# A hybrid retention/attention block on one Trainium2 core: a GpSimd adding transfer issued later, two slab loads swapped, and a VectorE norm put ahead of a slab sum

## The chip, the cores and the metric

One Trainium2 chip, one of its cores, one launch. The metric is the device time of the whole program in microseconds (us), lower is better. "Before" is the kernel as it stood, "after" the kernel with the diff below. All times are from the hardware profiler or from the device's own timing of a run.

## The reference, cut to what matters

```python
h    = rms_norm(x, norm1_g)                     # x: 256 x 2048, float32
proj = h @ w_in                                 # 2048 x 7168; columns: retention q,k,v,gate, attention q,k,v; 8 heads of 128 each
A = silu(gate) * head_group_norm(retention(rotary(q), rotary(k), v))
B = chunk_attention(rms_norm(aq), rms_norm(ak), av, rel_bias)     # chunks of 64 frames, softmax
x = x + concat(A, B) @ w_out                    # 2048 x 2048
x = x + square(relu(rms_norm(x, norm2_g) @ w_ff1)) @ w_ff2        # 2048 x 8192, 8192 x 2048
```

## The kernel before, in words

**Split products.** Every product is made in three: each float32 operand is split into a high part (fp32r) and a low part, and the matmuls high*high, low*high and high*low are added in PSUM. So every weight slab goes through four hands: SP (SyncE) issues its load into one of five raw buffers, ScalarE (ACT) writes the rounded copy `w_hi` (line 1095 in the first phase), VectorE (DVE) writes `w_lo = raw - w_hi` (line 1557), and TensorE (PE) does the matmuls of lines 840 and 847 (with `w_hi`) and of line 853 (with `w_lo`). A slab is four 128-row tiles, and is worked on in two halves called pieces, numbered q in the order of use.

**Phases.** The first phase, about 0 to 370 us, is the projection by `w_in`, head pair by head pair, with retention and attention of the finished heads between its pieces. Then come the product by `w_out` and the feed-forward. The change is in the first phase only.

**Blocks.** The first phase has four blocks of two heads, 0 to 3, and a remainder. `IN_STARTS` holds each block's first piece: 0, 26, 70, 114, 158. The function `at_piece(i, pos, f, ...)` puts a step f behind piece `IN_STARTS[i] + pos` in one engine's own order. ACT and DVE each run two pieces ahead (`AHEAD = 2`): at place q they first make the high or low half of piece q + 2 and then do the steps that are listed for q, in the order in which the lines list them. Each engine has such a list, and works it off strictly in order.

**Slab steps.** Within a block the slabs have names. I0 to I3 and J0 to J3 are the attention heads' slabs (384 columns), one set for each head. The retention pair's slabs are 512 columns wide and are multiplied in seven products instead of eight (Strassen's scheme): Q1 uses slab a, P5 uses a + b, P6 uses a + b + d, P7 uses b with a fourth slab added, P3 uses d, and so on. The same scheme in small letters (q1, p5, ...) serves a pair of attention heads. In blocks 1 to 3 the order of the last steps is I2 q2 Q1 I3 p4 P5 J2 P6 J3 P7 P3. These are at places 22 to 43 of the block, two places each, so J2 is at 34 and 35 and P6 at 36 and 37.

**Sums.** `in_sum(n, other, read)` on DVE adds a whole slab, 128x2048, to slab a (line 1566): first b, then d. The ACT copy of P6's first piece waits for the second of these sums (`in_summed >= 2 * pair + 2`). The fourth retention slab is added to b by a transfer that accumulates: `add_b` on GpSimd (POOL) waits for the first sum and then issues it (line 598); P7 waits for it to land. `add_e` does the same for slab a.

**Loads.** `IN_LOADS` is the order of SP's loads, and `in_plan` gives each the raw buffer that comes free first. Each load waits until DVE has made the low half of the last step that reads the buffer's earlier slab. In blocks 1 to 3 slab d waits for q2 and J2 waits for I3.

**Steps of the two heads.** Attention: ACT evacuates the projection with the scale 1/rms (`att_proj`, line 1115) and sums squares (`att_squares`, line 1131), DVE adds the epsilon (`att_mean_squares`, line 1645), POOL raises to the power -1/2 (`att_power`, line 588), DVE multiplies (`att_norm`, line 1650), PE transposes (`att_T`, line 701) behind place 35 of the block, directly ahead of P6. Retention of the second head of the pair before: `ret_power` on POOL (line 592) waits for statistics from DVE. The rotated q and k (`ret_rotated`, line 1696) are transposed by PE in `ret_T` (line 730).

**Block 0.** It has the same parts with fewer steps. The first norm's sums of squares of x are ACT's `x_squares` (line 1248); DVE's `x_mean_squares` and a POOL power make `rstd1`, which the first `att_proj` waits for. Product P5 is copied out of PSUM by `keep_in_p5` on ACT (line 1196).

Of the kernel before, what the change touches and what calls it, by code (L numbers as in the profile page):

```python
# [50 lines left out]
IN_STARTS = [0]  # L51
for _i in range(1, BLOCKS + 1):
    _r, _here = "Z1 Q2 Z2 P4 H1 H2", "Z1 Q2 q1 Z2 P4 p5 H1 p6 H2 p7 p3 I2 q2 Q1 I3 p4 P5 J2 P6 J3 P7 P3"
    _loads = "Z1 e A Z2 B D H1 H2 I2 E a I3 b d J2 J3" if _i < BLOCKS else "Z1 e Z2 H1 H2"
    IN_STARTS.append(2 * len(IN_ORDER))
    _before = ["Z1", "Q2", "Z2", "P4", "H1", "H2", "e"]
    IN_ORDER += [(_i - (step in _before), step) for step in (_here if _i < BLOCKS else _r).split()]
    IN_LOADS += [(_i - (name in _before), name) for name in _loads.split()]
# [28 lines left out]
def hybrid_block(nc, x, x_cols, w_att, w_ret, w_out, w_up, w_down, gains, rel_windows, rope_cos, rope_sin, decay, out):  # L87
# [3 lines left out]
    with ExitStack() as ctx:  # L91
# [486 lines left out]
        @block.gpsimd  # L578
        def _(pool):
            nc.gpsimd.memset(neg_half[:], -0.5).then_inc(half_ok, 1)  # L580
            nc.gpsimd.memset(ident[:], 0.0).then_inc(zeroed, 1)
            pool.wait_ge(zeroed, 1)
            nc.gpsimd.affine_select(out=ident[:], in_=ident[:], compare_op=ALU.not_equal, fill=1.0, base=0,
                                    pattern=[[-1, P]], channel_multiplier=1).then_inc(ident_ok, 1)

            def att_power(h):
                pool.wait_ge(a_ms_ok, h + 1)
                nc.gpsimd.tensor_tensor(a_rs[:], a_ms[:], neg_half[:], ALU.pow).then_inc(a_rs_ok, 1)

            def ret_power(u):  # L590
                pool.wait_ge(r_ve_ok, u + 1)
                nc.gpsimd.tensor_tensor(r_rs[:], r_ve[:], neg_half[:, 0:MT], ALU.pow).then_inc(r_rs_ok, 1)

            def add_second(n, into, c, done):

                table, cols = w_att if n % 2 else w_ret, SLAB_KT * pair_cols(n)
                row = pair_row(n, c, 1)
                nc.gpsimd.dma_start(raw[:, pair_raw(n, into)[0], 0:cols], table[row:row + P, :],
                                    accum_op=ALU.add).then_inc(done, 16)

            def add_b(n):
                pool.wait_ge(in_summed, 2 * n + 1)
                add_second(n, "b", 1, in_b)

            def add_e(n):
                pool.wait_ge(lo_done, pair_first(n, "P6") + 2)
                add_second(n, "a", 0, in_e)

            def mask_bias(i):
                pool.wait_ge(bias_in[i], 16)  # L610
                nc.gpsimd.memset(bias[0:CHUNK, 2 * i:2 * i + 2, P + CHUNK:2 * P], -1e30).then_inc(mask_ok, 1)

            add_b(0)
            pool.wait_ge(half_ok, 1)
            pool.wait_ge(me_ok, 1)
            nc.gpsimd.tensor_tensor(rstd1[:], me[:], neg_half[:, 0:MT], ALU.pow).then_inc(rstd1_ok, 1)
            att_power(0)
            mask_bias(0)
            add_e(0)
            att_power(1)  # L620
            for i in range(1, BLOCKS):
                add_b(2 * i - 1)
                add_e(2 * i - 1)
                ret_power(2 * i - 2)
                mask_bias(i)
                add_b(2 * i)
                ret_power(2 * i - 1)
                att_power(2 * i)
                add_e(2 * i)
                att_power(2 * i + 1)  # L630
            ret_power(HEADS - 2)
            ret_power(HEADS - 1)

            def add_slabs(p):

                table, first = weights(p)
                pool.wait_ge(summed, 2 * p + 1)
                row = ((first + 1) * SLABS + 1) * P
                nc.gpsimd.dma_start(raw[:, PLAN[p, "b"][0], :], table[row:row + P, :],
                                    accum_op=ALU.add).then_inc(b_summed, 16)  # L640
                pool.wait_ge(slab_lo, slab_no(p, "P6") + 1)
                row = (first * SLABS + 1) * P
                nc.gpsimd.dma_start(raw[:, PLAN[p, "a"][0], :], table[row:row + P, :],
                                    accum_op=ALU.add).then_inc(e_summed, 16)

            add_slabs(0)
            pool.wait_ge(me2_ok, 1)
            nc.gpsimd.tensor_tensor(rstd2[:], me2[:], neg_half[:, 0:MT], ALU.pow).then_inc(rstd2_ok, 1)
            for p in range(1, PAIRS):
                add_slabs(p)  # L650
# [6 lines left out]
        def _(pe):  # L657
# [213 lines left out]

            for h in range(HEADS):
                i, second = h // 2, h % 2
                places = ((23, 25, 27, 28), (29, 31, 34, 36))[second] if i == 0 else (
                    (35, 37, 41, 43), (46, 48, 51, 53))[second]
                for pos, f in zip(places, (att_T, att_scores, att_PT, att_pv)):
                    at_piece(i, pos, f, h)
# [188 lines left out]
        def _(act):  # L1066
# [191 lines left out]
            def at_piece(i, pos, f, *args):  # L1258
                work.setdefault(IN_STARTS[i] + pos, []).append(lambda: f(*args))

            for f, pos in enumerate((9, 11, 18, 20)):
                at_piece(0, pos, s_hi, f)
            for c, pos in enumerate((14, 15, 16, 17)):
                at_piece(0, pos, x_squares, c)
            at_piece(0, 12, keep_in_q1, 0)
            at_piece(0, 16, keep_in_p5, 0)
            at_piece(0, 18, att_proj, 0)
            at_piece(0, 20, att_squares, 0)
            at_piece(0, 22, att_proj, 1)
            at_piece(0, 23, att_qT, 0)  # L1270
# [5 lines left out]
            at_piece(0, 28, att_mix, 0)  # L1276
            at_piece(0, 30, att_qT, 1)
            at_piece(0, 32, att_exp, 1)
            at_piece(0, 35, att_pT, 1)
            at_piece(0, 37, att_mix, 1)  # L1280
            for i in range(1, BLOCKS):
                h, u, n = 2 * i, 2 * i - 2, 2 * i
                at_piece(i, 6, keep_in_q1, n - 1)
# [267 lines left out]
        def _(dve):  # L1551
# [17 lines left out]
            def in_sum_half(n, other, read, half):  # L1569
# [6 lines left out]
                if half:  # L1576
                    ins.then_inc(in_summed, 1)

            def set_z(n):

                dve.wait_ge(p5_kept, n + 1)
                dve.wait_ge(piece_used, pair_first(n, "P6") + 2)
                dve.wait_ge(acc_read_act, pair_reads(n) + 1)
                cols = slice(0, pair_cols(n))
                nc.vector.tensor_tensor(bZ[:, cols], in_p5[:, cols], bX[:, cols], ALU.subtract).then_inc(z_set, 1)
# [182 lines left out]
            def at_piece(i, pos, f, *args):  # L1768
                work.setdefault(IN_STARTS[i] + pos, []).append(lambda: f(*args))
# [6 lines left out]
                at_piece(0, pos, s_lo, f)  # L1776
            at_piece(0, 10, in_sum, 0, "b", "Q1")
            at_piece(0, 14, in_sum, 0, "d", "P5")
            at_piece(0, 17, x_mean_squares)
            at_piece(0, 19, set_z, 0)  # L1780
            at_piece(0, 19, s_lo, 2)
            at_piece(0, 20, att_mean_squares, 0)
# [6 lines left out]
            at_piece(0, 28, att_norm, 1)  # L1789
            at_piece(0, 32, att_bias_max, 1)  # L1790
            at_piece(0, 32, att_probs, 1)
            at_piece(0, 37, att_mix, 1)
            for i in range(1, BLOCKS):
                h, u, n = 2 * i, 2 * i - 2, 2 * i
                at_piece(i, 3, in_sum, n - 1, "b", "Q1")
                at_piece(i, 8, in_sum_half, n - 1, "d", "P5", 0)
                at_piece(i, 9, in_sum_half, n - 1, "d", "P5", 1)
                at_piece(i, 9, ret_rotate, u)
                at_piece(i, 11 if i == 1 else 10, ret_rotated, u)
                at_piece(i, 13, ret_kT, u)  # L1800
                at_piece(i, 14, ret_decay, u)
                at_piece(i, 16, set_z, n - 1)
                at_piece(i, 17, ret_norm, u)
                at_piece(i, 19, set_w, n - 1)
                at_piece(i, 20, ret_rotate, u + 1)
                at_piece(i, 21, ret_mix, u)
                at_piece(i, 21, ret_rotated, u + 1)
                at_piece(i, 24, ret_kT, u + 1)
                at_piece(i, 25, in_sum, n, "b", "Q1")
                at_piece(i, 26, ret_decay, u + 1)  # L1810
                at_piece(i, 29, ret_norm, u + 1)
                at_piece(i, 31, in_sum, n, "d", "P5")
                at_piece(i, 32, att_mean_squares, h)
                at_piece(i, 33, ret_mix, u + 1)
                at_piece(i, 34, att_norm, h)
                at_piece(i, 38, set_z, n)
                at_piece(i, 38, att_bias_max, h)
                at_piece(i, 40, att_probs, h)
                at_piece(i, 41, set_w, n)
                at_piece(i, 42, att_mean_squares, h + 1)  # L1820
                at_piece(i, 44, att_mix, h)
                at_piece(i, 44, att_norm, h + 1)
                at_piece(i, 49, att_bias_max, h + 1)
                at_piece(i, 50, att_probs, h + 1)
                at_piece(i, 54, att_mix, h + 1)
# [314 lines left out]
```

## Time and profile before

| | |
|---|---|
| median of 3 runs | 1103.39 us (1102.66 to 1103.53) |
| the profiled execution | 1103.28 us, span of the core 1101.1 us |
| PE busy | 1090.8 us (99%) |
| DVE busy | 885.7 us (80%) |
| ACT busy | 715.8 us (65%) |
| POOL busy | 59.2 us (5%) |
| granted TensorE clock | full in every slice |
| chain that ended last | PE 89%, DVE 3%, DMA 2%, ACT 1% |

The span is what the profile covers, from the first instruction to the last; the execution's time is 2.2 us more. Busy times of PE are of matmuls whose ends are modelled. An engine's idle time is put down to what ended it, and idle time of ACT, DVE or POOL costs nothing unless PE waits in its turn.

### The profile page before, as it was taken

The numbers are of one execution on the slowest core, as the hardware profiler recorded it, in microseconds if no ns is written. First come the engines' busy times: TensorE is split into PE (matmuls) and PEld (weight loads), VectorE is DVE, ScalarE is ACT, GpSimd is POOL, SyncE is SP. The second block draws the span as 40 slices with busy tenths as digits, with TensorE's granted clock in tenths as the row PEclk, the third lists the DMA queues.
The fourth block names the chain that finished last, engine by engine and source line by source line (L and its number), as shares of the span: only waits on it lengthen the run. The fifth ranks groups of instructions, "written<-read, shape, count | busy, mean of one in ns | idle before, by whom it ended". The sixth has DMA issues, their size and how long they took to land.

```text
span 1101.1 us, 13180 instructions
## 1 busy us (share of the span) xinstructions
PE 1090.8 (99%) x5154; PEld 925.1 (84%) x5154; DVE 885.7 (80%) x836; ACT 715.8 (65%) x857; POOL 59.2 (5%) x75
## 2 busy tenths in 40 slices
PE   9999999999999999999999999999999999999998
PEld 9788889889888888888888888888888888888887
DVE  7888878988976677969878779778869787869784
ACT  7876676776764456777755677655677655577662
POOL 0100100100100000000000000000000000000000
PEclk9999999999999999999999999999999999999999
DMA  9886776776756647778788788787787787787792
GB/s 362 298 262 218 214 261 218 227 249 229 226 211 252 256 159 219 257 249 251 230 282 244 253 267 231 229 302 223 249 285 217 238 290 223 258 278 220 246 279 91
DMA packets 44829, 268.53 MB, mean 244 GB/s; under 512 B 4960, under 2 KB 7776, under 8 KB 17120
## 3 DMA queue, kind: packets, MB, share of 16 engines
q1 hardware_dynamic: 37712, 220.61, 53.6%
q0 software_dynamic: 6624, 46.66, 22.4%
q8 instruction: 41, 0.67, 0.2%
q10 hardware_dynamic: 432, 0.41, 0.1%
q14 instruction: 20, 0.16, 0.0%
HBM read 265.57 MB, written 2.10 MB: 243 GB/s over the span
## 4 chain that ended last, share of the span: by engine, by line
PE 89%; DVE 3%; DMA 2%; ACT 1%; issue 1%; DVEq 0%; ACTq 0%
PE acc L972 10%; PE acc L968 10%; PE acc L970 10%; PE acc L840 5%; PE acc L847 5%; PE acc L853 5%; PE bankC L930 4%; PE bankC L923 4%; PE acc L930 4%; PE acc L923 4%; PE acc L925 4%; PE bankC L925 4%; DMA raw<-in_w_att 2%; PE acc L668 2%; PE acc L673 2%; PE acc L680 2%
## 5 line engine op out<-in xcount | busy, mean ns | idle before, releaser
L1867 DVE TENSOR_TENSOR w_lo<-raw,w_hi 128x2048 fp32r<-128x2048 f32 x180 | 410.9, 2288 | 127.2 <-ACT w_hi L1360 126.9
L1360 ACT ACTIVATE w_hi<-raw 128x2048 fp32r<-128x2048 f32 x180 | 344.7, 1916 | 219.8 <-PE acc L972 150.6
L1557 DVE TENSOR_TENSOR w_lo<-raw,w_hi 128x1024 fp32r<-128x1024 f32 (+1 forms) x168 | 180.8, 1093 | 36.9 <-ACT w_hi L1095 36.4
L1095 ACT ACTIVATE w_hi<-raw 128x1024 fp32r<-128x1024 f32 (+1 forms) x168 | 156.8, 954 | 39.6 <-PE acc L853 22.4
L968 PE MATMUL acc<-w_hi,hF_hi 128*128 128x512 f32 x256 | 100.8, 394 | 0.0
L972 PE MATMUL acc<-w_hi,hF_lo 128*128 128x512 f32 x256 | 99.8, 390 | 0.0
L970 PE MATMUL acc<-w_lo,hF_hi 128*128 128x512 f32 x256 | 99.7, 389 | 0.0
L968 PE MATMUL acc<-w_hi,dF_hi 128*128 128x512 f32 x248 | 96.8, 391 | 0.0
L972 PE MATMUL acc<-w_hi,dF_lo 128*128 128x512 f32 x248 | 96.5, 389 | 0.0
L970 PE MATMUL acc<-w_lo,dF_hi 128*128 128x512 f32 x248 | 96.5, 389 | 0.0
L840 PE MATMUL acc<-w_hi,hT_hi 128*128 128x384 f32 (+1 forms) x336 | 87.3, 374 | 3.0 <-ACT w_hi L1095 2.8
L847 PE MATMUL acc<-w_hi,hT_lo 128*128 128x384 f32 (+1 forms) x336 | 83.3, 362 | 0.0
L853 PE MATMUL acc<-w_lo,hT_hi 128*128 128x384 f32 (+1 forms) x336 | 83.0, 361 | 0.2 <-DVE w_lo L1557 0.2
L1875 DVE TENSOR_TENSOR raw<-raw 128x2048 f32<-128x2048 f32 x32 | 73.1, 2284 | 0.0
L840 PEld LDWEIGHTS acc<-w_hi,hT_hi 128*128 128x128 f32 x336 | 59.2, 188 | 9.8 <-ACT w_hi L1095 5.0
L853 PEld LDWEIGHTS acc<-w_lo,hT_hi 128*128 128x128 f32 x336 | 61.2, 188 | 7.1 <-DVE w_lo L1557 0.6
L847 PEld LDWEIGHTS acc<-w_hi,hT_lo 128*128 128x128 f32 x336 | 61.5, 188 | 6.8
L972 PEld LDWEIGHTS acc<-w_hi,hF_lo 128*128 128x128 f32 x256 | 48.1, 188 | 10.1
L968 PEld LDWEIGHTS acc<-w_hi,hF_hi 128*128 128x128 f32 x256 | 48.1, 188 | 9.8
L970 PEld LDWEIGHTS acc<-w_lo,hF_hi 128*128 128x128 f32 x256 | 48.1, 188 | 9.5
L972 PEld LDWEIGHTS acc<-w_hi,dF_lo 128*128 128x128 f32 x248 | 46.6, 188 | 9.7
L970 PEld LDWEIGHTS acc<-w_lo,dF_hi 128*128 128x128 f32 x248 | 46.6, 188 | 9.6
(278 smaller groups left out, 1903.1 us busy)
## 6 DMA issues: line engine op xcount, KB each, us to landing
raw<-in_w_up SPq DMA_DIRECT2D x64, 1024.0 KB, 6.2
raw<-in_w_down SPq DMA_DIRECT2D x64, 1024.0 KB, 6.5
raw<-in_w_ret SPq DMA_DIRECT2D x32, 1024.0 KB, 6.0
raw<-in_w_att SPq DMA_DIRECT2D x28, 768.0 KB, 5.8
raw<-in_w_out SPq DMA_DIRECT2D x16, 1024.0 KB, 4.8
raw<-in_w_up POOLq DMA_DIRECT2D x16, 1024.0 KB, 9.1
raw<-in_w_down POOLq DMA_DIRECT2D x16, 1024.0 KB, 8.7
raw<-in_w_ret POOLq DMA_DIRECT2D x8, 1024.0 KB, 9.2
```

Of the source, the lines that this page charges most:

```text
L840: nc.tensor.matmul(bank[:, 0:wide], stationary(step, m, t)[0], piece(w_hi, q, start, start + wide), start=fresh, stop=False, skip_group_ch ...
L847: nc.tensor.matmul(bank[:, 0:n], stationary(step, m, t)[1], piece(w_hi, q, start, start + n), start=False, stop=False, skip_group_check=True)
L853: mm = nc.tensor.matmul(bank[:, 0:n], stationary(step, m, t)[0], piece(w_lo, q, start, start + n), start=False, stop=t == SLAB_KT - 1, ski ...
L923: nc.tensor.matmul(bank[:], hi[:, form, tile_cols(t)], wh[:, cols], start=first and t == 0, stop=False, skip_group_check=True)
L925: nc.tensor.matmul(bank[:], lo[:, form, tile_cols(t)], wh[:, cols], start=False, stop=False, skip_group_check=True)
L968: nc.tensor.matmul(banks[m][:], hi[:, form + m, tile_cols(t)], wh[:, cols], start=False, stop=False, skip_group_check=True)
L970: nc.tensor.matmul(banks[m][:], hi[:, form + m, tile_cols(t)], wl[:, cols], start=False, stop=False, skip_group_check=True)
L972: mm = nc.tensor.matmul(banks[m][:], lo[:, form + m, tile_cols(t)], wh[:, cols], start=False, stop=t == SLAB_KT - 1, skip_group_check=True)
L1095: nc.scalar.activation(piece(w_hi, q, 0, n), raw[:, r, half * n:(half + 1) * n], ACT.Copy).then_inc(hi_done, 1)
L1360: nc.scalar.activation(w_hi[:, ring(s)], raw[:, r, :], ACT.Copy).then_inc(slab_hi, 1)
L1557: nc.vector.tensor_tensor(piece(w_lo, q, 0, n), raw[:, IN_PLAN[i, READ_AT.get(step, step)][0], half * n:(half + 1) * n], piece(w_hi, q, 0, ...
L1867: nc.vector.tensor_tensor(w_lo[:, ring(s)], raw[:, r, :], w_hi[:, ring(s)].bitcast(f32), ALU.subtract).then_inc(slab_lo, 1)
```

## The change

In block 0 it reorders ACT's steps between places 16 and 20, puts the copy of P5 on DVE (`keep_first_p5`), and moves the second head's `att_pT`, `att_pv` and `att_mix` one place forward. In blocks 1 to 3 it loads J2 ahead of d, issues `add_b` behind `ret_power` of the second head and behind the landing of J2, moves DVE's sum with d from place 31 to 33 and its `att_norm` from 34 to 33, ahead of that sum. In block 1 `ret_rotated` goes from place 11 to 10, as in the other blocks.

```diff
-    _loads = "Z1 e A Z2 B D H1 H2 I2 E a I3 b d J2 J3" if _i < BLOCKS else "Z1 e Z2 H1 H2"
+    _loads = "Z1 e A Z2 B D H1 H2 I2 E a I3 b J2 d J3" if _i < BLOCKS else "Z1 e Z2 H1 H2"
...
+            def slab_landed(i, name):
+                slot, loaded, _ = IN_PLAN[i, name]
+                pool.wait_ge(in_raw[slot], loaded)
...
                 mask_bias(i)
+                ret_power(2 * i - 1)
+                slab_landed(i, "J2")
                 add_b(2 * i)
-                ret_power(2 * i - 1)
                 att_power(2 * i)
...
-                places = ((23, 25, 27, 28), (29, 31, 34, 36))[second] if i == 0 else (
+                places = ((23, 25, 27, 28), (29, 31, 34, 35))[second] if i == 0 else (
...
-            for f, pos in enumerate((9, 11, 18, 20)):
+            for f, pos in enumerate((9, 11, 19, 20)):
                 at_piece(0, pos, s_hi, f)
-            for c, pos in enumerate((14, 15, 16, 17)):
+            for c, pos in enumerate((14, 15, 17, 18)):
                 at_piece(0, pos, x_squares, c)
             at_piece(0, 12, keep_in_q1, 0)
-            at_piece(0, 16, keep_in_p5, 0)
-            at_piece(0, 18, att_proj, 0)
+            at_piece(0, 19, att_proj, 0)
...
-            at_piece(0, 35, att_pT, 1)
-            at_piece(0, 37, att_mix, 1)
+            at_piece(0, 34, att_pT, 1)
+            at_piece(0, 36, att_mix, 1)
...
+            def keep_first_p5():
+                dve.wait_ge(piece_used, pair_first(0, "P5") + 2)
+                nc.vector.tensor_copy(in_p5[:], bF[:]).then_inc(p5_kept, 1)
...
-            at_piece(0, 17, x_mean_squares)
+            at_piece(0, 16, keep_first_p5)
+            at_piece(0, 18, x_mean_squares)
...
-            at_piece(0, 37, att_mix, 1)
+            at_piece(0, 36, att_mix, 1)
...
-                at_piece(i, 11 if i == 1 else 10, ret_rotated, u)
+                at_piece(i, 10, ret_rotated, u)
...
-                at_piece(i, 31, in_sum, n, "d", "P5")
                 at_piece(i, 32, att_mean_squares, h)
                 at_piece(i, 33, ret_mix, u + 1)
-                at_piece(i, 34, att_norm, h)
+                at_piece(i, 33, att_norm, h)
+                at_piece(i, 33, in_sum, n, "d", "P5")
```

## Rows read from the trace of the kernel before

**Rows 1.** Waits of PE, whole span: waiting line, releaser, total us, times, longest us.

```profile
PE acc L840 <- ACT w_hi L1095: 2.8, 3, 1.4
...
PE bankC L840 <- ACT w_hi L1095: 1.2, 1, 1.2
PE bankA L730 <- DVE r_qk L1696: 0.9, 1, 0.9
PE bankA L701 <- DVE a_qk L1650: 0.5, 1, 0.5
```

**Rows 2.** Timeline of PE, block 1, P5 to P6: start us, us, instructions, idle before.

```profile
121.88 0.63 PE L853 MATMUL bankD<-w_lo,sf_hi 128*128 128x512 f32 x2
123.94 0.97 PE L840 MATMUL acc<-w_hi,hT_hi 128*128 128x384 f32 x4 [1.43 <-ACT w_hi L1095]
...
128.59 0.71 PE L840 MATMUL bankC<-w_hi,sf_hi 128*128 128x512 f32 x2
```

**Rows 3.** Timeline of SP, block 1: issues of b and d, then of J2 and J3.

```profile
104.17 3.06 SPq L484 DMA_DIRECT2D raw<-in_w_ret  x2
114.31 2.06 SPq L484 DMA_DIRECT2D raw<-in_w_att  x2
```

**Rows 4.** Timeline of ACT, block 1, around the copy of J2.

```profile
120.76 0.19 ACT L1131 ACTIVATION_READ_ACCUMULATOR junk<-a_proj_first 128x1 f32 x1
123.04 1.58 ACT L1095 ACTIVATE w_hi<-raw 128x768 fp32r<-128x768 f32 x2 [2.09 <-DMA raw<-in_w_att]
```

**Rows 5.** Timeline of DVE, block 1: sum with d, J2's first low half, mix, norm.

```profile
120.57 2.29 DVE L1566 TENSOR_TENSOR raw<-raw 128x2048 f32<-128x2048 f32 x1
123.92 0.96 DVE L1557 TENSOR_TENSOR w_lo<-raw,w_hi 128x768 fp32r<-128x768 f32 x1 [1.06 <-ACT w_hi L1095]
...
125.73 0.48 DVE L1733 SCALAR_TENSOR_TENSOR zT_lo<-bankA,gv,zT_hi 128x256 fp32r<-128x256 f32 x1
...
127.26 0.68 DVE L1650 TENSOR_TENSOR a_qk<-a_proj_first,a_rs 128x512 f32<-128x512 f32 x1
```

**Rows 6.** Timeline of POOL, blocks 0 and 1: att_power, add_b, ret_power, att_power.

```profile
50.73 1.02 POOL L588 TENSOR_TENSOR a_rs<-a_ms,neg_half 128x4 f32<-128x4 f32 x1 [5.36 <-DVE a_ms L1645]
...
112.38 0.91 POOL L598 DMA_DIRECT2D raw<-in_w_ret  x1 [14.74 <-DVE raw L1566]
117.41 0.71 POOL L592 TENSOR_TENSOR r_rs<-r_ve,neg_half 128x2 f32<-128x2 f32 x1 [4.13 <-DVE r_ve L1722]
125.04 1.65 POOL L588 TENSOR_TENSOR a_rs<-a_ms,neg_half 128x4 f32<-128x4 f32 x1 [6.92 <-DVE a_ms L1645]
```

**Rows 7.** Tile raw, 104 to 128 us: durations in ns, min/median/max; DMA to landing.

```profile
L1557 DVE TENSOR_TENSOR w_lo<-raw,w_hi x15: 947/953/1226, 103.2 to 127.9; 128x768 fp32r<-128x768 f32 x9, 128x1024 fp32r<-128x1024 f32 x6
L1095 ACT ACTIVATE w_hi<-raw x15: 830/847/1060, 103.4 to 127.3; 128x768 fp32r<-128x768 f32 x9, 128x1024 fp32r<-128x1024 f32 x6
...
DMA to landing us min/median/max: 4.7/6.8/9.2
```

**Rows 8.** DMA issues of 29.9 to 30.2 us (slab J3, block 0): KB, us to landing.

```profile
raw<-in_w_att SPq DMA_DIRECT2D x1, 768.0 KB, 13.0
```

**Rows 9.** Timeline of ACT, block 0: last squares of x, copy of J3, first evacuation.

```profile
42.63 0.62 ACT L1248 ACTIVATE junk<-xq 128x512 f32<-128x512 f32 x1
...
44.01 0.83 ACT L1095 ACTIVATE w_hi<-raw 128x768 fp32r<-128x768 f32 x1
...
45.46 1.06 ACT L1115 ACTIVATE a_proj_first<-acc,rstd 128x384 f32<-128x384 f32 x2
```

**Rows 10.** Timeline around ret_T of block 1: PE, ACT, DVE, PE.

```profile
76.87 0.49 PE L716 MATMUL bankB<-ident,a_p 128*128 128x128 f32 x3
...
77.77 0.84 ACT L1095 ACTIVATE w_hi<-raw 128x768 fp32r<-128x768 f32 x1
...
82.30 2.35 DVE L1557 TENSOR_TENSOR w_lo<-raw,w_hi 128x1024 fp32r<-128x1024 f32 x2
...
85.64 0.44 PE L730 MATMUL bankA<-ident,r_qk 128*128 128x128 f32 x2 [0.87 <-DVE r_qk L1696]
```

## The prediction

> **What bounds the kernel now.** First the page's busy shares (the table above): PE is busy for 1090.8 of 1101.1 us at full clock, so an edit of the first phase can only touch the some 10 us in which it isn't. Then the waits of PE, which say who ends them [rows 1]. The largest group, 2.8 us in three waits, the longest 1.4, is PE waiting for ACT's high copy. The timeline of PE places the longest: behind P5 of block 1, ahead of J2 [rows 2]. The other two sit at the same place of blocks 2 and 3 and share the remaining 1.4. Then the timelines of the engines behind it. ACT had been idle for 2.09 us until a DMA landed, and only then copied J2 [rows 4]. SP had issued J2 at 114.31 [rows 3], so it took 8.7 us to land, and POOL had issued its adding transfer 1.9 us before it [rows 6]. The fastest landing of a weight slab in this stretch is 4.7 us, the slowest 9.2 [rows 7]. So here a DMA bounds PE, for 2.8 us in all. Elsewhere PE waits 0.9 us for DVE's rotated q and k in block 1, 0.5 us for the first norm and 1.2 us for P6 in block 0 [rows 1].
>
> **Part 1, J2 loaded ahead of d, add_b later.** J2 takes d's turn, the second of the two loads that begin at 104.17; that one is issued at 104.17 + 3.06 - 0.33, about 106.9 [rows 3]. Even at the slowest landing, 9.2 us [rows 7], it is there by 116.1, ahead of its copy. POOL's wait for it delays little: add_b now also stands behind the second retention power, which runs at 117.41 and ends at 118.12 [rows 6]. So the transfer goes out at 118.1 instead of 112.4 and lands by 127.3 at 9.2 us. P7 comes behind J2, P6 and J3, and a J slab alone keeps PE for over 4 us [rows 2], so its copy isn't wanted before some 130: hidden. Queued behind add_b is att_power, needed at 122.9 (below), so nothing waits there. d is issued at 114.31 without the adding transfer beside it. It lands between 119.0 (4.7 us) and 123.5 (9.2 us); I take 119 to 120, since what stood beside J2 is gone. The three waits go: **-2.8**.
>
> **Part 2, the sum with d behind the norm.** This is a new wait. I follow block 1 with PE no longer held. ACT is free at 120.95 [rows 4] and copies J2's first piece at once. DVE's low half started 0.88 after that copy did (123.04 to 123.92) [rows 4, 5], so now at 121.73. The mean squares come right behind it, and POOL's power started 1.12 after that low half did (123.92 to 125.04) and takes 1.65 [rows 5, 6]: from 122.85 to 124.50. DVE meanwhile ends the second low half and the mix; in the trace that is 125.73 + 0.48 - 123.92 = 2.29 behind the first low half [rows 5], so 124.02, and it waits 0.5 for POOL. Norm, 0.6 (0.68 less overlap), to 125.2; sum, 2.29, to 127.5 [rows 5]. Only then can ACT copy P6's first piece, 1.06 at most [rows 7]: PE can begin P6 at 128.6. When would PE want it? It is free at 121.88 + 0.63 = 122.51, and from J2's start to P6's start it needs 128.59 - 123.94 = 4.65 [rows 2]: at 127.15. So PE idles 1.45. The low half of P6 follows 1.23 behind the high copy [rows 7], but PE gets through the two groups of high matmuls in some 0.9: 0.3 more. In all 1.75 a block, and all three blocks have this order: **+5.2**. In the kernel before, this sum lay in the 2.3 us in which DVE would have waited for J2 anyway [rows 5]; that cover is given up.
>
> The least this can cost: without any wait for POOL the norm starts at 124.02, 0.5 earlier, so 1.25 a block, +3.8. The most: d lands at 123.5 (still ahead of the sum's start at 125.2, so free), and the wait at the low half comes out at twice my 0.3, so 2.05 a block, +6.2.
>
> Of POOL's power the trace shows two prices for the same 128x4: 1.02 at 50.73, and 1.65 at 125.04 [rows 6], where it starts during the subtraction of J2's second piece; blocks 2 and 3 repeat 1.65. The new order has the same instruction beside it, so 1.65 is taken. The Trainium skill, SBUF — State Buffer, section "Who interferes with whom", says that a VectorE instruction with two SBUF inputs holds off a GpSimd one that reads SBUF until it ends. By that rule the 1.65 stays and the time is my forecast; if the 1.65 had another cause and fell to 1.02, it would be 1104.3. The two rows agree with the rule.
>
> **Part 3, block 0.** ACT now has squares 2 behind the copy of P6's second piece, and J3's first copy ahead of squares 3. J3 is issued at 29.97 and takes 13.0 us: it lands at 43.0 [rows 8]. So squares 3 cannot start before 43.0 + 0.75 = 43.75, where they started at 42.63, and end ahead of the copy at 44.01, taking 1.38 [rows 9]. The mean, POOL's power and the evacuation hang on them: 1.1 later, 46.55 instead of 45.46 [rows 9]. One copy of 768 columns that used to lie behind the evacuation (0.75) is now ahead of it. So the chain of ACT up to P7's copy and then to DVE's first norm, for which PE waits already [rows 1], is later by 1.1 - 0.75: **+0.35**. Between +1.1 (if that copy doesn't come off) and -0.65 (if squares 3 found J3 landed early; the time saved on ACT by the copy of P5 then counts). The 1.2 us wait of PE at P6 shrinks, but the first norm is behind it and takes that back. The copy of P5 on DVE, some 0.7 by its nearest row (0.68 for 512 columns) [rows 5], lies in DVE's wait ahead of P6's second low half: free, or 0.3 if not.
>
> **Part 4, block 1's start.** DVE's rotated sum now comes after one low half instead of two (2.35 for the two [rows 10]): 1.13 earlier. But ACT's att_pT now stands ahead of the evacuation and the copy that ran at 77.77, and must wait for PE's transposes, until 76.87 + 0.49 = 77.36 [rows 10]. It takes some 0.4 (half of the 0.83 of a copy with twice its columns) and the evacuation 1.1 (1.06) [rows 9], so that copy moves to 78.9, by 1.1. DVE's low half follows it, and between 0 and 1.1 of the delay reaches the rotated sum; I take 0.7, since DVE had other work there. Net 0.4 earlier, and PE loses some 0.1 of it at the low half that it runs ahead of ret_T: **-0.3**; between -0.9 (the whole wait) and 0. PE's own move of att_pv is nothing: the same matmuls one place sooner.
>
> **Sum.** -2.8 + 5.2 + 0.35 - 0.3 = +2.4. On the profiled execution, 1103.28, which is 0.1 below the median of the runs, 1105.7. The terms' lower bounds give -2.8 + 3.8 - 0.65 - 0.9 = -0.55, the upper ones -2.8 + 6.2 + 1.4 = +4.8.
>
> **Rivals.**
> (a) Faster: P6 isn't late. The place is DVE's sum in blocks 1 to 3. If it ended by 126.0, P6's copy would be done by 127.1 and PE would not wait. Then the time is 1103.3 - 2.8 = 1100.5. For it: J2's wait surely goes, and the sum stood clear of PE before. Against: even if POOL cost nothing, low half, mix, norm and sum end at 127.0. It takes 1 us less than the rows show.
> (b) No change: DVE doesn't wait for POOL, and ret_T gains all of 0.9: -2.8 + 3.8 + 0.35 - 0.9 = +0.45, 1103.7. Against it is the repeated 1.65.
> (c) Much slower: the adding transfer, issued at 118.1 with J3 and the decay tables in flight, lands over 3 us later than 9.2, so that P7's copy waits too. Block 0 shows 13.0 us for a slab in a crowded queue [rows 8]. Some 1 us a block more: 1108.5. Against: here the queue empties by 125.
>
> **How the numbers follow.** About 0.2% (2.2 us) is what a measurement of this kernel can tell from no change, so faster is below 1101.2 and slower above 1105.6. The forecast has 0.69; its own range is 1104.3 to 1107.3, and a little over half of that lies above 1105.6. Rival (a) has 0.06, (b) 0.14, (c) 0.11. Slower: 0.41 + 0.11 = 0.52. Same: 0.28 + 0.14 = 0.42. Faster: 0.06. The range leaves out (a) and the end of (c): 1103.2 to 1107.8.
>
> **What the profile after would show.** Right: no PE wait at J2; in each of blocks 1 to 3 a PE wait on ACT's copy at P6 (bankC, line 840), about 1.4, and a short one at line 853; ACT idle until DVE's sum of line 1566 there; att_norm ahead of that sum, released by POOL; the adding transfer at 118; the first evacuation at 46.5; the wait at ret_T about 0.5. Wrong: the sum over before 126; no bankC wait but those of block 0; a wait for in_w_ret at P7; or the DVE chain starting earlier than 121.7, since ACT was free sooner than I take it.

## The result, and the profile after

| | before | after |
|---|---|---|
| median of the runs, us | 1103.46 (1102.66 to 1103.61, 6 runs) | 1108.50 (1107.82 to 1109.18, 6 runs) |
| ratio, 95% interval | | 1.0038 [1.0027, 1.0048] |
| profiled execution, us | 1103.28 | 1108.56 |
| its span, us | 1101.1 | 1106.8 |
| its mean granted clock | 1.0 | 0.998 |

The changed kernel is slower by 5.0 us by its medians, where +2.4 was forecast; 1108.50 lies 0.7 above the top of the range. By the ratio it is 4.2 us, which would still be inside (the range ends 4.4 above the median before); the quotient of the two medians, 1.0046, lies in the ratio's interval. The unaltered change measured twice more, below, gave 4.5 and 4.2. So the loss is certain, and its size is 4 to 5 us. The first lines of its page, and its chain of work that ended last:

```profile
span 1106.8 us, 13183 instructions
PE 1094.2 (99%) x5154; PEld 926.0 (84%) x5154; DVE 887.0 (80%) x837; ACT 714.1 (65%) x856; POOL 59.0 (5%) x75
...
PE 88%; DVE 6%; ACT 3%; issue 2%; DMA 1%; POOL 0%; SPq 0%; ACTq 0%; DVEq 0%
```

PE's waits over the whole span (the columns of [rows 1]; the change moves line 840 to 845, 853 to 858, 1095 to 1100, 1557 to 1561, 1566 to 1570, 1645 to 1653):

```profile
PE bankC L845 <- ACT w_hi L1100: 5.0, 4, 1.5
...
PE bankC L858 <- DVE w_lo L1561: 1.0, 1, 1.0
PE acc L858 <- DVE w_lo L1561: 0.9, 1, 0.9
PE bankA L706 <- DVE a_qk L1658: 0.5, 1, 0.5
```

The three waits at J2 ([rows 1], first line) are gone. In their place stand three at P6, 4.3 us of the 5.0 (the fourth, of 0.6, is block 0's, 1.2 before). The 1.0 on bankC for a low half is new and is block 0's too. The wait for the rotated q and k, 0.9 before, is gone, but the low half just ahead of it is now waited for 0.9, where that was 0.2.

The chain of work through block 1 of the changed kernel, 121 to 132 us (start, us, what), shows how P6 came to be late:

```profile
121.51 0.74 ACT w_hi L1100
122.25 0.02 issue
122.28 0.96 DVE w_lo L1561
123.24 0.09 DVE a_ms L1653
123.33 0.08 issue
123.41 1.67 POOL a_rs L588
125.08 0.02 issue
125.10 0.04 DVE a_qk L1658
125.14 0.57 issue
125.71 2.30 DVE raw L1570
128.01 0.02 issue
128.03 1.06 ACT w_hi L1100
```

It is the chain of the forecast's part 2 link by link: J2's copy, its low half, the mean squares, POOL's power, the norm, the sum with d, and only then P6's copy. DVE's timeline has the wait of the norm for POOL:

```profile
125.10 0.69 DVE L1658 TENSOR_TENSOR a_qk<-a_proj_first,a_rs 128x512 f32<-128x512 f32 x1 [0.53 <-POOL a_rs L588]
```

PE stood meanwhile (its timeline, block 1, columns of [rows 2]):

```profile
129.14 0.73 PE L845 MATMUL bankC<-w_hi,sf_hi 128*128 128x512 f32 x2 [1.44 <-ACT w_hi L1100]
129.71 0.62 PE L852 MATMUL bankC<-w_hi,sf_lo 128*128 128x512 f32 x2
130.40 0.81 PE L858 MATMUL bankC<-w_lo,sf_hi 128*128 128x512 f32 x2
131.01 1.06 PE L845 MATMUL bankC<-w_hi,sf_hi 128*128 128x512 f32 x2
```

**The clock.** The last group has the form of the first, and takes 1.06 where that took 0.73. The windows of that stretch (start:end, length, busy time and count of PE, PEld, DVE, ACT and POOL, granted clock, DMA share, GB/s):

```profile
129.00:130.00 1.00, 0.86 (x4) 0.67 (x4) 0.88 (x1) 1.00 (x3) 0.00 (x0) 1.00 1.03 434
130.00:131.00 1.00, 0.94 (x4) 0.48 (x3) 0.79 (x2) 1.00 (x2) 0.00 (x0) 0.95 0.52 205
131.00:132.00 1.00, 1.00 (x4) 0.81 (x3) 1.00 (x2) 1.00 (x4) 0.00 (x0) 0.50 0.02 8
...
133.00:134.00 1.00, 1.00 (x5) 0.82 (x5) 1.00 (x2) 0.85 (x2) 0.00 (x0) 0.50 0.96 90
134.00:135.00 1.00, 1.00 (x6) 0.93 (x6) 1.00 (x2) 0.87 (x1) 0.00 (x0) 0.84 0.59 98
```

For 3.4 us, behind the 1.44 us gap and with PE busy again, the granted clock is 0.50, so 1.2 GHz of the 2.4. It comes once in this execution. Before, the clock was full from end to end.

**Where the 5 us are.** Both kernels run the same 5154 matmuls in the same order except for a few near att_pv, so the starts of the same matmul can be compared. How much later the profiled execution of the changed kernel is than that of the kernel before, worked out from the two traces:

| at | later, us | since the row above |
|---|---|---|
| 12 us (startup, which the change doesn't touch) | +0.71 | |
| P6's second piece, block 0, 42.8 us | -0.67 | -1.38 |
| first norm, block 0 | +0.86 | +1.53 |
| ret_T, block 1 | +0.53 | -0.33 |
| J2, block 1 | -1.14 | -1.67 |
| P6, block 1 | +0.90 | +2.04 |
| behind the stretch at half clock | +2.51 | +1.61 |
| J2, block 2 | +1.63 | -0.88 |
| P6, block 2 | +3.69 | +2.06 |
| att_PT, block 2 | +4.07 | +0.38 |
| J2, block 3 | +2.98 | -1.09 |
| P6, block 3 | +5.04 | +2.06 |
| att_PT, block 3 | +5.33 | +0.29 |
| ret_y of the remainder, 335 us | +5.75 | +0.42 |
| end | +5.65 | -0.10 |

The spans differ by 5.7. The startup's 0.71 is not carried on: the kernel before waits 1.2 us ahead of P6's second piece in block 0 [rows 1], the changed one doesn't and is ahead there. The variant with the loads alone, further below, shows the same: 1.1 late at 12 us, 0.2 early at the first norm. So the 0.86 arises in block 0 itself, where the first evacuation comes later (ACT's timeline; 45.46 before [rows 9]):

```profile
47.05 1.05 ACT L1120 ACTIVATE a_proj_first<-acc,rstd 128x384 f32<-128x384 f32 x2
```

How much of it is the change's is less sure. In the eight traces with the change's order of block 0 the first norm stands 0.71 to 1.28 later than in the kernel before, in the five others -0.16 to +1.30.

The 0.42 at 335 us has its own cause, in SP's timeline and ACT's:

```profile
334.50 1.95 SPq L465 DMA_DIRECT2D raw<-in_w_out  x4
...
339.45 1.06 ACT L1076 ACTIVATE w_hi<-raw 128x1024 fp32r<-128x1024 f32 x1 [2.67 <-DMA raw<-in_w_out]
```

The kernel before has these lines instead, from SP, with no such wait of ACT:

```profile
310.59 14.71 SPq L465 DMA_DIRECT2D raw<-in_w_out  x2
324.97 1.28 SPq L465 DMA_DIRECT2D raw<-in_w_out  x3
```

`in_plan` gives each slab the buffer that comes free first, so the swap of two loads permutes the buffers of all later ones. By that plan the last steps to read buffers 0 to 4 are 80, 83, 82, 81, 84 before and 84, 80, 81, 82, 83 after. The first slab of w_out always goes to buffer 0 and stands first in SP's queue. It now waits for the very last step, and all the others wait behind it. Numbered alike, PE's starts go back by 0.13 to 0.37 at this place in all nine traces with the swap and the old w_out slots (the changed kernel's is the largest), and by 0.00 in the three with the old loads and in the one, below, where w_out's slabs go to the buffers that are free first.

### The profile page after: what moved, and what is told of

Read it like the earlier page. It is cut to its first block, busy times and chain, and to the rows that moved or that the text cites. A ratio compares the mean times of both kernels' runs of the same rounds, so it can differ in the third digit from the quotient of the medians.

```text
span 1106.8 us, 13183 instructions
## 1 busy us (share of the span) xinstructions
PE 1094.2 (99%) x5154; PEld 926.0 (84%) x5154; DVE 887.0 (80%) x837; ACT 714.1 (65%) x856; POOL 59.0 (5%) x75
## 4 chain that ended last, share of the span: by engine, by line
PE 88%; DVE 6%; ACT 3%; issue 2%; DMA 1%; POOL 0%; SPq 0%; ACTq 0%; DVEq 0%
PE acc L977 10%; PE acc L973 10%; PE acc L975 10%; PE acc L845 4%; PE acc L852 4%; PE acc L858 4%; PE bankC L935 4%; PE acc L935 4%; PE acc L930 4%; PE bankC L930 4%; PE bankC L928 4%; PE acc L928 4%; DVE w_lo L1561 3%; PE acc L673 2%; PE acc L678 2%; PE acc L685 2%
```

## The experiments

Two theories first. A: the sum's place behind the norm makes P6 late, and that is the whole loss; all else in the change is a gain of some 3 to 4 us. B: moving the sum matters little, and the loss lies in the swapped transfers. All ratios are against the kernel before on the same chip; its median was 1104.22 beside the first four runs (26 executions), 1103.88 beside the next four (9) and 1104.04 beside the last four (17).

**The change with the sum back at its old place.**

```diff
-                at_piece(i, 33, att_norm, h)
-                at_piece(i, 33, in_sum, n, "d", "P5")
+                at_piece(i, 31, in_sum, n, "d", "P5")
+                at_piece(i, 34, att_norm, h)
```

> The changed kernel with DVE's sum with d back at place 31 and att_norm back at 34; loads, POOL's order and block 0 as changed. Theory A (the sum stands too late, P6 waits for it): with d landing at about 120 the sum again fits into DVE's idle time ahead of J2's low half. The three bankC waits of about 1.45 us go, and so does the half-clock stretch of 3.4 us behind the first of them. J2's waits stay away too, so it is faster than the kernel before by 3 to 4 us: 1099.5 to 1100.5. Theory B (the late adding transfer or POOL's wait for J2 is what costs): P6 or P7 still waits for a transfer in blocks 1 to 3, and the time stays above 1104.

Measured: 1101.08 (1100.72 to 1101.74, 7 runs), 0.9974 [0.9964, 0.9985]. That is 0.6 above what A expected, and far from B's 1104. So some 7 us hang on this one edit, and the rest of the change is a gain. DVE in block 1 of this run:

```profile
121.50 2.29 DVE L1570 TENSOR_TENSOR raw<-raw 128x2048 f32<-128x2048 f32 x1
...
127.04 0.69 DVE L1658 TENSOR_TENSOR a_qk<-a_proj_first,a_rs 128x512 f32<-128x512 f32 x1
```

The sum starts 4.2 us earlier than in the changed kernel, and the norm has no wait for POOL in front of it. PE waits nowhere in blocks 1 to 3 but once 0.9 ahead of ret_T. All seven runs have full clock.

**Both at place 33, the sum ahead of the norm.**

```diff
+                at_piece(i, 33, in_sum, n, "d", "P5")
                 at_piece(i, 33, att_norm, h)
-                at_piece(i, 33, in_sum, n, "d", "P5")
```

> The changed kernel with the sum with d directly ahead of att_norm, both at place 33. Theory A: the sum starts when the mix ends, 1.15 us earlier, and no longer waits for POOL's power. P6's wait falls from 1.44 to 0.3 or 0.4 a block, PE waits 0.3 to 0.5 for the norm ahead of att_T instead. With a gap that small the clock stays up. 1108.5 - 3 x 0.8 - 1.7 = 1104.4, between 1103.5 and 1105. Theory B: no change, 1108 or more. If the clock still falls behind a short gap, some 1106.

Measured: 1103.54 (1103.32 to 1103.9, 10 runs), 0.9991 [0.9982, 1.0001]. DVE and then POOL in block 1:

```profile
124.67 2.28 DVE L1570 TENSOR_TENSOR raw<-raw 128x2048 f32<-128x2048 f32 x1
126.87 0.68 DVE L1658 TENSOR_TENSOR a_qk<-a_proj_first,a_rs 128x512 f32<-128x512 f32 x1
```

```profile
123.59 1.66 POOL L588 TENSOR_TENSOR a_rs<-a_ms,neg_half 128x4 f32<-128x4 f32 x1 [3.92 <-DVE a_ms L1653]
```

The sum covers POOL's 1.66 us here, instead of standing behind it, and PE waits only for the norm, 0.5 in three blocks. The time is some 5 us below the change's; all ten runs have full clock, so 1.1 or so of that is the clock. The sum is still 3.2 us later than at place 31, and that costs 2.5 us over three blocks. So both the later place and the norm ahead of it cost. The time is what A expected (1103.5 to 1105), and theory A stands.

**The change without the edits of POOL.**

```diff
+                add_b(2 * i)
                 ret_power(2 * i - 1)
-                slab_landed(i, "J2")
-                add_b(2 * i)
```

> The changed kernel with add_b ahead of ret_power of the second head again and without POOL's wait for J2; the rest as changed. Theory A: d now shares the queues with the adding transfer and lands at 123 to 124 instead of 120, still ahead of the sum's start at 125.7. P6's wait stays at 1.4 and the time at 1108.5 within 0.5. Theory B (the later adding transfer costs): faster by over 1 us, 1107.5 or less. If d lands past 125.7, P6's wait grows by as much.

Measured: 1107.28 (1107.11 to 1107.77, 7 runs), 1.0029 [1.0019, 1.0040]; the same kernel again, as e11, with its expectation:

> The kernel with add_b early (first of the two for the clock), again, beside the changed kernel on one chip. Theory C (whether the half-clock stretch comes depends on chip and launch): it shows it as often as the changed kernel does. Theory D' (it hangs on the later adding transfer as well as on P6's wait): never here, in most runs there. Time without the stretch 1107.3, with it 1108.5.

1107.02 (1106.81 to 1107.65, 6 runs), 1.0027 [1.0016, 1.0038]. d takes longer to land when the adding transfer is ahead of it (DMA issues at 115 us: KB, us to landing; first this run, then the change):

```profile
raw<-in_w_ret SPq DMA_DIRECT2D x1, 1024.0 KB, 9.7
```

```profile
raw<-in_w_ret SPq DMA_DIRECT2D x1, 1024.0 KB, 6.1
```

It lands at 124.7, ahead of the late sum, so this costs nothing here. The P6 waits are those of the change (4.9 us in four, longest 1.4). But none of the 13 executions has a stretch at half clock. So the change without that stretch is a kernel of some 1107.1 to 1107.5, and the stretch is worth the last 1.1 or so. By its number alone the first of these runs missed A's 1108.5 within 0.5 and met B's 1107.5 or less; but the waits that B would take away are all there, and what is missing is the stretch. Why the stretch stays away with the early transfer is not shown.

**The order of block 0 alone, on the kernel before.** The squares, mean squares, first evacuation and the copy of P5 on DVE, as in the change; `att_pT`, `att_pv` and `att_mix` stay.

> The kernel before with the change's order of ACT between places 16 and 20 of block 0, the P5 copy on DVE and the mean squares at 18, nothing else. Prediction part 3: squares 3 stand behind J3's landing at 43.0, the first evacuation starts 1.1 us later, less 0.75 for a copy made earlier: +0.2 to +0.4, 1103.6 to 1103.9. Rival: block 0 carries a large share of the +5.0, 1105 or more. Other rival: it gains, since PE's 1.2 us at P6 shrinks: 1102.5.

Measured: 1104.15 (1103.75 to 1105.78, 10 runs), 0.9999 [0.9990, 1.0008]: no loss is seen, but the interval reaches 0.9 us up, so it can't tell the forecast's +0.35 from nothing. It does rule out that block 0 is a large share of the loss.

**The swap of the loads alone, on the kernel before.**

```diff
-    _loads = "Z1 e A Z2 B D H1 H2 I2 E a I3 b d J2 J3" if _i < BLOCKS else "Z1 e Z2 H1 H2"
+    _loads = "Z1 e A Z2 B D H1 H2 I2 E a I3 b J2 d J3" if _i < BLOCKS else "Z1 e Z2 H1 H2"
```

> The kernel before with J2 loaded ahead of d and nothing else: add_b is issued at 112.4 as before, the sum with d stays at place 31. J2's waits go (-3.4). d now shares the queues with the adding transfer, lands at 123 instead of 111, and DVE waits for it at place 31 with J2's low half behind it: the sum ends at 125.4, PE waits at line 853 of J2 for about 1.9 a block and at att_T for 0.5. +4 in all, 1108. Rival: d lands by 121 since it is first in its queue; then faster by 2 to 3. This tells whether the later adding transfer is needed for the swap of the loads.

Measured: 1113.21 (1112.78 to 1113.65, 4 runs), 1.0085 [1.0071, 1.0099]: 9.3 us slower, where some 4 were expected. DVE and PE in block 1:

```profile
123.87 2.29 DVE L1566 TENSOR_TENSOR raw<-raw 128x2048 f32<-128x2048 f32 x1 [3.58 <-DMA raw<-in_w_ret]
```

```profile
127.09 1.65 PE L853 MATMUL acc<-w_lo,hT_hi 128*128 128x384 f32 x4 [3.33 <-DVE w_lo L1557]
```

The slab that now stands second, d, lands 9.7 us after its issue. The sum at place 31 waits for it, DVE does J2's low half only behind the sum, and PE waits 3.33. The group of four matmuls takes 1.65, where the same form takes 0.97 in [rows 2]: again the clock, 0.50 for 3.4 us from about the end of each of the three long waits (3.33, 2.28 and 2.26) in the profiled execution. The mean clock is 0.995 in all four. So on the swap alone both the waits and the clock were mis-sized, and the swap needs the later adding transfer.

**The later adding transfer alone, on the kernel before.** This is the counterpart: one line moved, the loads in their old order, no wait for J2.

```diff
-                add_b(2 * i)
                 ret_power(2 * i - 1)
+                add_b(2 * i)
```

> The kernel before with add_b behind ret_power of the second head and nothing else: the loads, the sum and the norm stay. The adding transfer then goes out at 118 instead of 112, and J2, issued at 114.3, has the queues to itself. Theory A (J2 was late because of the adding transfer beside it, not because of its place in the order): J2 lands in some 5 us, at 119 to 120, before its copy; its three waits of 3.4 us in all go without any swap of the loads, less 1.0 for the norm behind one more low half. 1101.5 to 1100.5, ratio 0.9975. Theory E (J2 has to be loaded ahead of d): J2 still lands after 121.7 and at least half of the waits stay, 1102.5 or more.

Measured: 1101.18 (1100.39 to 1102.32, 11 runs), 0.9975 [0.9966, 0.9984]. SP, POOL and ACT in block 1, each from its timeline:

```profile
115.57 2.06 SPq L484 DMA_DIRECT2D raw<-in_w_att  x2
```

```profile
119.31 0.91 POOL L598 DMA_DIRECT2D raw<-in_w_ret  x1
```

```profile
122.14 1.56 ACT L1095 ACTIVATE w_hi<-raw 128x768 fp32r<-128x768 f32 x2
```

J2 is issued 6.6 us ahead of its copy and lands in 5.4, where it took 8.7 before; the copy finds it landed. There is no wait at J2, with the loads not swapped at all. So J2 need not be loaded ahead of d; what made it late was the adding transfer of 1 MB issued 1.9 us ahead of it [rows 3, 6]. The swap is superfluous once that is gone.

**The unaltered change, twice more**, for the state of its clock:

> The changed kernel once more, unaltered, beside runs of the kernel before on the same chip. The question is the half-clock stretch of 3.4 us behind P6's first long wait, which the kernel with add_b early (same waits of 1.4 us) did not show in any run. Theory C (the stretch is a matter of the chip and the launch, not of this schedule): here too it is missing in most runs, and the kernel is slower than before by 3.0 to 3.5 us. Theory D (the schedule of the change brings it on): nearly every run shows a mean clock of 0.998, slower by 4.5 to 5.5 us.

> The changed kernel, unaltered, on the same chip as the run above: mean clock 0.998 and 1108.4 in most runs by theory D', and 1.0 and 1107.1 as often as above by theory C.

Measured: 1108.39 (1107.09 to 1108.52, 4 runs), 1.0042 [1.0027, 1.0057], and 1108.21 (1107.38 to 1109.15, 4 runs), 1.0039 [1.0025, 1.0052]. In the profiled one of the second the stretch at half clock lies in another block, behind P6's wait of block 2:

```profile
215.00:216.00 1.00, 1.00 (x4) 0.71 (x3) 1.00 (x2) 1.00 (x3) 0.33 (x1) 0.50 0.00 0
```

Over all 14 executions of the changed kernel 10 have a mean clock of 0.998 and take 1108.1 to 1109.2 us; four have 1.0 and take 1107.1 to 1107.8. The half-clock stretch came in three of four and in two of four executions here, so neither "nearly every run" nor "missing in most" describes it.

**What is worth keeping.** Three kernels were put together from the parts that gain. The swap of loads and POOL's new order, with the sum at 31, the norm at 34 and block 1's earlier rotated sum (place 10, with block 0's second att_mix at 36):

> The kernel before with the swap of the loads, POOL's new order, ret_rotated at 10 with att_mix at 36, and nothing of block 0's order, the P5 copy, the sum and the norm; att_pT stays at 35 and att_pv at 36. J2's waits go: -3.4. ret_T's wait goes whole, since ACT no longer waits for the transposes ahead of two tasks: -1.0. att_T waits 0.3 a block for a norm behind one more low half, as with the sum at 31: +1.0. w_out's first slab gets a buffer that comes free later: +0.3. -3.1 in all, and block 0's changes are worth nothing: 0.9970 of before. Rival: att_mix at 36 with att_pT at 35 holds ACT so long that ret_T still waits: 0.9977.

1100.26 (1099.62 to 1100.72, 5 runs), 0.9967 [0.9954, 0.9979]. The wait at ret_T is gone from PE's waits, and the one at its low half is 0.2 as in the kernel before, while the change had only traded one for the other. Its difference from the change there is att_pT, which stays at 35 in block 0: ACT then evacuates and copies first. That this is what does it wasn't tried alone. The same with the norm at 33 and w_out in the buffers that are free first:

> The kernel above with att_norm at 33 (the sum with d stays at 31) and with the slabs of w_out in raw buffers 1 to 4 instead of 0 to 3, in the order in which the swapped loads free them. Norm ahead of P6's low half takes att_T's wait of 0.3 a block away (-0.6 to -1.0) and, since the sum is long done, doesn't hold P6. The loads of w_out go out as early as before: -0.3. In all 0.9 to 1.3 faster than the kernel above: 0.9960. Rival: the norm's wait for POOL now holds P6's low half, and PE waits at line 853 instead: no gain over the kernel above.

1099.82 (1099.44 to 1100.33, 5 runs), 0.9965 [0.9952, 0.9977]. In the traces it gains 0.65 us on the run above, behind ret_T, where 0.9 to 1.3 were expected; in the times the two can't be told apart. Last, without the swap of loads, and so with the old buffer plan:

```diff
-                add_b(2 * i)
                 ret_power(2 * i - 1)
+                add_b(2 * i)
...
-            at_piece(0, 37, att_mix, 1)
+            at_piece(0, 36, att_mix, 1)
...
-                at_piece(i, 11 if i == 1 else 10, ret_rotated, u)
+                at_piece(i, 10, ret_rotated, u)
...
-                at_piece(i, 34, att_norm, h)
+                at_piece(i, 33, att_norm, h)
```

(att_mix is moved on ACT and on DVE.)

> The kernel above with ret_rotated at 10 and att_mix at 36 (-1.0) and att_norm at 33 (-0.6 to -1.0), loads in the old order. If theory A holds, this reaches or beats the fastest kernel so far with four small edits and no change of buffers: ratio 0.9960 to 0.9965, 1099.5 to 1100. Under theory E: 0.9980 or more.

Measured: 1099.29 (1099.17 to 1099.49, 5 runs), 0.9958 [0.9945, 0.9970]: 4.7 us faster than the kernel before, some 9 faster than the change, and the best of all that ran. Its waits of PE, then DVE in block 1:

```profile
PE bankC L840 <- ACT w_hi L1095: 1.2, 1, 1.2
PE bankA L701 <- DVE a_qk L1650: 0.5, 1, 0.5
PE acc L853 <- DVE w_lo L1557: 0.2, 1, 0.2
```

```profile
119.77 2.29 DVE L1566 TENSOR_TENSOR raw<-raw 128x2048 f32<-128x2048 f32 x1
...
124.80 0.69 DVE L1650 TENSOR_TENSOR a_qk<-a_proj_first,a_rs 128x512 f32<-128x512 f32 x1 [0.53 <-POOL a_rs L588]
```

The norm waits the same 0.53 us for POOL as in the changed kernel. But the sum is done by then, so nobody waits for the norm.

## Why the prediction was right and where it fell short

The direction, the mechanism and the place were right. By its own steps:

- **J2's waits, -2.8.** They went. J2 was issued at 107.45 (forecast 106.9). By starts the three gave -3.64: PE lost 0.2 to 0.3 more at each wait than the idle time that the profile lists. The reason that the text gave, the adding transfer ahead of it, was right, but it treated the swap as the cure; the one-line run shows that the later transfer alone is enough.
- **P6, +5.2.** Idle 1.44 against 1.45 forecast; POOL's power 1.66 against 1.65; DVE's wait for it 0.53 against 0.5; the norm's end at 125.7 and the sum's at 128.0, each 0.5 later than forecast, as this execution already is by 0.53 at ret_T. (Two slips in the text cancel: 120.95 + 0.88 is 121.83, not 121.73, and 124.50 + 0.6 is 125.1, not 125.2.) By starts it is 2.05 a block and not 1.75: 1.68 at the wait, which is listed as 1.44, and 0.36 at the low half, for which 0.3 was taken. The three make 6.16, close to the +6.2 of the text's upper bound, but that bound had put the excess at the low half. J2 and P6 together: +2.5 measured, +2.4 forecast; that both were short by 0.8 to 1.0 and cancel is luck.
- **d at 119 to 120.** It landed 6.1 us after 114.85, at 121.0, with no effect, as the text said for any time up to 125.
- **The adding transfer**, issued at 118.6, took 11.2 us and not 9.2, to 129.8; P7's copy didn't wait, so rival (c) did not occur, though its 1108.5 is the time that came.
- **Block 0, +0.35.** The first evacuation stands at 47.05 (46.55 forecast), and PE is 0.86 late at the first norm. The copy of P5 on DVE is not free either: the low half of P6's second piece starts when it ends, and PE waits 1.0 for that; the first norm is waited for all the same. The run with this part alone can't tell +0.35 from nothing.
- **ret_T, -0.3.** Measured -0.33. DVE's rotated sum came 0.4 earlier and PE lost 0.1 of it at the low half, as the text had it; but the text left 0.5 of waiting at ret_T, and the trace has none there and 0.9 at the low half ahead.
- **POOL's rule.** The Trainium skill, SBUF — State Buffer, section "Who interferes with whom", let one expect the 1.65 to stay beside DVE's subtraction; the trace agrees (1.65 or 1.66, in every run with that neighbour), and the time by the other reading, 1104.3, didn't come.

What failed is the sum itself, which had only the edits' own places in it. Three terms are missing:

1. **The clock, +1.6** in the profiled execution. The text took the new gaps of 1.45 us at their length. Some of them cost a stretch of 3.4 us at 1.2 GHz besides. In 10 executions of 14 this came once; the other four, at 1107.1 to 1107.8, show the change without it: +3.2 to +4.4 against the medians beside them, in the upper part of the range. Against the one profiled execution of the change at full clock the stretch is worth 1.3 by the end, since it hides the next term in its own block.
2. **att_PT, +0.67** in blocks 2 and 3. DVE's low halves bunch up behind the late sum, and the probabilities that PE transposes come later. The text followed the late sum to P6 and no further. The traces at hand settle where it comes from: PE loses some 0.3 a block there in every one of the six with the sum at place 33, also where it stands ahead of the norm (but for the blocks with a half-clock stretch), and 0.0 in the seven with the sum at 31.
3. **w_out's buffers, +0.42.** The text read the swap as two loads in each other's place, and not as a new assignment of all buffers behind them. No term stood for it, and there was no rival for it either.

To the forecast's +2.4 these add 1.6, 0.7 and 0.4, and block 0's 0.86 is 0.5 more than its term: +5.6, against 5.7 between the spans. Between the profiled executions it is 5.3, since what lies outside the span is 0.4 less in the changed one (1.8 us for 2.2). The 5.0 and 4.2 of the medians and the ratio are smaller still: not every execution has the stretch, and the first norm of block 0 varies by over 1 us between traces with its old order. So the agreement is one of two executions and not of the medians.

## What to carry to other kernels

Where a sum or a conversion sits in time that its engine would spend waiting anyway, moving it behind something that waits for a third engine costs twice: the cover is given up, and that wait stands in front of it as well. Before one reorders loads, one asks what was in flight beside the late one: moving the transfer that shared the queues was worth 2.9 us by itself, and the swap worth nothing but a permuted buffer plan whose bill came 200 us later. And a new gap of over a microsecond on TensorE is priced with what the clock may take behind it, not by its length alone.

## What the runs showed of the hardware

- **A gap can cost a stretch at half clock, but not surely.** Behind the gaps of 2.3 to 3.3 us at J2 (the loads alone) the stretch of 3.4 us at clock 0.50 came three times in the profiled execution, and the mean clock of all four is 0.995. Behind gaps of 1.4 us it came once in 10 of 14 executions of the change (by the mean clock), and in none of 13 of the variant with an early adding transfer, whose gaps are as long. The kernel before, whose longest wait is 1.4 as well, has a mean clock of 0.998 in 5 of the 52 executions run beside the experiments, and they are among its slowest (1105.4 to 1106.2); the run with the adding transfer alone has it once in 11, behind a wait of 1.6 at P6 of block 0. What decides between these stays open. One such stretch of the changed kernel is worth 1.1 us between the means of its executions with and without it, and 1.3 between the traces.
- **An adding transfer slows the loads beside it by half or more.** 1 MB: 9.7 us beside it, 6.1 without. 768 KB: 8.7 beside it [rows 3, 4], 5.4 for the same load with that transfer moved. The adding transfer itself took 8.8 to 11.5 us for 1 MB in blocks 1 to 3.
- **The idle time that the profile lists is less than what PE lost.** Waits listed as 0.6 to 1.45 us moved the starts behind them by 0.2 to 0.3 more. At J2 that made 3.64 where 2.8 is listed; at P6 it made 5.1 where 4.3 is listed, and the low half that follows, for which nothing is listed, brought it to 6.16.
